# Long convolution in eight channel groups: ScalarE's scaled copy issued one frequency block ahead, VectorE's product ahead of the sums, and the decay table in three transfers

## The chip, the cores and the metric

One NeuronCore of a Trainium2 chip runs the whole program once. The metric is device time in microseconds (us) of one execution; the runs of a kernel are compared by their median. Engines are named as in the profile: PE is TensorE's matmul, PEld its weight load, DVE VectorE, ACT ScalarE, POOL GpSimd, SP the engine that issues most transfers.

## The reference, cut to what matters

The program computes two blocks of a network with long convolutions, attention and experts. The change lies in one part of the first block, the bidirectional long convolution of the first mixer. Its filters are implicit: a small net gives values per position, a last matrix (`f_w4`) and a decay table turn them into taps for each of 2048 channels, forward and backward, and each channel is divided by the sum of the taps' magnitudes.

```python
filt = (hdn @ w4.astype(F32)).reshape(T, 2, D_INNER)
filt = filt * jnp.exp(-t * deltas[None, :])[:, None, :]
filt = filt / (jnp.sum(jnp.abs(filt), axis=(0, 1), keepdims=True) + HY_FILTER_EPS)
...
y = jnp.fft.irfft(jnp.fft.rfft(vf, n=n, axis=1) * jnp.fft.rfft(taps, n=n, axis=0)[None],
                  n=n, axis=1)[:, :T]
return (y + vf * skip.astype(F32)).astype(v.dtype)
```

T is 528 and `v` is the product of two streams that the part before has projected and convolved briefly.

## The kernel before, in words

Everything is float32. A matmul operand is split into a high and a low part (`hi_part` on ScalarE, `lo_part` on VectorE or GpSimd), and three matmuls (`mm3`, lines 93 to 95) stand for one. The Fourier transforms are matmuls with cosine and sine matrices (`mats_h`, `mats_l`), made small by folding the signal and the filter into even and odd halves.

The 2048 channels are worked in eight groups `c` of 256. Within a group there are five frequency blocks `z`; the first four have 128 frequencies, the fifth has 57. For each block TensorE transforms the signal (`signal`), then one piece of the next group's filter product (`taps`), then the filter (`freq`). `tensor_conv` fixes that order, and behind the fifth block come the inverse transforms (`tensor_back`), and the sums for the next group's norm (`tensor_filter_end`, line 1058). A group n = c + 1 has its filter made while group c is transformed: three tiles `i` of positions (128, 128 and 41), each in two steps `m`, six steps in all. All six go through one PSUM bank, so each `taps` waits for the VectorE product `hp` (line 1005) of the step before it.

The names that the later steps touch are:

- `hp`, `vector_filter`, line 1005: VectorE's product of filter and decay table, PSUM to SBUF. The second step of a tile also waits for `abs0` of that tile.
- `abs0` and `abs`, `scalar_filter`: ScalarE's magnitudes of the first and second step. In the trace `abs0` is `sq<-hp`, and `abs` is `dec<-hp`, since it overwrites the decay table. For the first tile ScalarE also halves one row (`hp<-hp`), which the small sum of line 1014 (1 partition, 256 columns) needs.
- `fsum`, `vector_differ`, line 1021: VectorE's sum and difference of the taps of one tile.
- `vector_larger`, line 1027: VectorE's maximum of the two magnitudes.
- `hc`, `scalar_freq`: ScalarE's scaled copy of the transformed filter (in the trace `hc<-ps,wf`). It waits for TensorE's filter transform of that block.
- `prods`, `vector_freq`, line 1198: VectorE's product of signal and filter transform, and behind it the two sums `rr` of lines 1204 and 1205. TensorE's signal transform two blocks later waits for `prods`, since it reuses the bank.
- `Y_h`, `scalar_product`: ScalarE's high part of `rr`; `Y_l` is GpSimd's low part of it. `yh` and `yl` are the same for a finished group of outputs.
- `w4s`, `w4h`, `w4l`: sum and difference of the last matrix's halves (VectorE), high part (ScalarE) and low part (GpSimd), for the filter products two groups ahead.
- `dec`: the decay table of a group, 768 KB, fetched by SP as soon as the norm's sums of the group before are done.

Every engine runs its own list of instructions in the order in which the loops `scalar_conv`, `vector_conv`, `gpsimd_conv` and `tensor_conv` write them. One semaphore per engine counts its steps in this part (`cv.vec`, `cv.act` and so on), so an instruction that waits holds all behind it on its engine. The head of group 0 is made inside the part before (`vector_head`, `scalar_head`).

Of the kernel before, what the change touches and what calls it, by code (L numbers as in the profile page):

```python
# [140 lines left out]
def build(nc, stack, I, C, out):  # L141
# [782 lines left out]
    def sync_conv(e, w):  # L924
        w.wait_ge(*lo_by(HEAD - 2))
        e.dma_start(dec[:], C["dec"][0]).then_inc(*land("dec", 0))
        sync_w4(e, w, 1)
        for c in range(1, 8):
            w.wait_ge("cv.pe", "norm", c - 1)
            e.dma_start(dec[:], C["dec"][c]).then_inc(*land("dec", c))  # L930
            if c < 7:
                sync_w4(e, w, c + 1)
        n = first["hyo", 0]
        filters_over(w)
        sync_weights(e, w, n)
        w.wait_ge("cv.pe", "freq", 7, 4)
        sync_weights(e, w, n + 2)
# [58 lines left out]
    def vector_filter(e, w, c, step):  # L996
# [4 lines left out]
        w.wait_ge("dec", c)  # L1001
# [132 lines left out]
    def tensor_freq(e, w, c, z, part):  # L1134
# [15 lines left out]
        w.wait_ge("left" if z == 4 else "tl")  # L1150
# [76 lines left out]
    def tensor_back_end(e, w, c, h):  # L1227
# [3 lines left out]
        w.wait_ge("left")  # L1231
# [99 lines left out]
    def scalar_conv(e, w):  # L1331
        scalar_unit(e, w, (7, 3, 1), hy_step[7, 3, 1])
        scalar_sums(e, w, 0)
        scalar_w4(e, w, 1)
        for c in range(8):
            for z in range(5):
                if c + z == 0:
                    scalar_freq(e, w, 0, 0)
                if c < 7:
                    scalar_filter(e, w, c + 1, z if z < 4 else 5)  # L1340
                if c + z:
                    scalar_freq(e, w, c, z)
                if c < 7 and z == 4:
                    scalar_turned(e, w, c + 1)
                elif c == 7 and z == 2:
# [16 lines left out]
    def vector_head(e, w, x):  # L1362
# [12 lines left out]
        elif x == (7, 3, 0):  # L1375
# [4 lines left out]
            vector_differ(e, w, 0, 2)  # L1380
            vector_larger(e, w, 0, 2)

    def vector_conv(e, w):
# [3 lines left out]
        vector_w4(e, w, 1)  # L1387
        for c in range(8):
            n = c + 1
            for z in range(5):  # L1390
                if c + z == 0:
                    vector_freq(e, w, 0, 0)
                if c < 7:
                    vector_filter(e, w, n, z if z < 4 else 5)
                    if z in (1, 3):
                        vector_differ(e, w, n, z // 2)
                    if z == 3:
                        vector_filter(e, w, n, 4)
                    elif z == 4:
                        vector_differ(e, w, n, 2)  # L1400
                if c + z:
                    vector_freq(e, w, c, z)
                if c < 7 and z in (1, 3):
                    vector_larger(e, w, n, z // 2)
# [29 lines left out]
    def gpsimd_conv(e, w):  # L1434
# [12 lines left out]
        e.dma_start(tl_x[:], C["tl"]).then_inc(*land("tl"))  # L1447
# [4 lines left out]
        e.dma_start(flat(lf[0][:]), C["lf"][0]).then_inc(*land("left"))  # L1452
        e.dma_start(lb_x[:], C["lb"]).then_inc(*land("left"))
        gpsimd_w4(e, w, 1)
        hyena_over(w)
        e.dma_start(flat(lf[1][:]), C["lf"][1]).then_inc(*land("left"))
# [3013 lines left out]
```

## Time and profile before

| | us |
|---|---|
| median of 3 runs (2398.54 to 2405.86) | 2405.53 |
| the profiled execution | 2406.78 |
| its span | 2405.0 |

The profiled execution is the one whose trace is read below; its time holds 1.8 us that lie outside the span.

| engine | busy us | share of the span |
|---|---|---|
| PE | 2236.0 | 93% |
| PEld | 1855.4 | 77% |
| DVE | 1367.0 | 57% |
| ACT | 1004.5 | 42% |
| POOL | 618.4 | 26% |

The shares are means over the whole program. The long convolution of this change takes the stretch from about 411 to 714 us of the span. In the trace a group of channels starts where its first `vT_h,mats_h` matmul does; the groups 1 to 6 lie between 459.28 and 687.60 us. In a row of the order of time the first number is the start in us from the span's start, the second the duration in us, and brackets hold the idle time of the engine before the row with what ended it.

### The profile page before, as it was taken

The page shows a single profiled execution, that of the slowest core. Times are in us where ns is not written, and L with a number is a line of the kernel's source. Part 1 is how long each engine was busy: PE and PEld are TensorE (multiplying, and loading weights), DVE is VectorE, ACT ScalarE, POOL GpSimd, SP SyncE. Part 2 cuts the span into 40 slices and gives each one's busy share as a digit, 9 for nine tenths or more (in the row PEclk, how much of TensorE's full clock was granted, in tenths as well). Part 3 has the DMA queues.
Part 4 walks back from the last instruction along what each step waited for, and adds up shares of the span by engine and source line. Part 5 has one row for each costly group of instructions (what it writes and reads, how often), then busy time and mean ns, then how long its engine had stood idle before and what let it go on. Part 6 is the DMA issues. An engine that isn't in the chain of part 4 may idle for free.

```text
span 2405.0 us, 36878 instructions
## 1 busy us (share of the span) xinstructions
PE 2236.0 (93%) x15305; PEld 1855.4 (77%) x15305; DVE 1367.0 (57%) x2335; ACT 1004.5 (42%) x1832; POOL 618.4 (26%) x520
## 2 busy tenths in 40 slices
PE   7999999898999989999999989889989999699998
PEld 7999999888999989899999867856776677333332
DVE  4455546788872566666666667789455664411112
ACT  4344334444432455655656553435433432211112
POOL 1111123555541132322323201203220111133331
PEclk9999999899999999999999989999988999799999
DMA  5322332110014223222222224312331143799993
GB/s 182 103 74 88 101 116 79 44 36 19 32 54 135 62 69 82 71 74 78 72 69 80 54 53 102 103 36 75 86 113 49 32 126 116 268 367 376 371 377 145
DMA packets 226337, 274.78 MB, mean 114 GB/s; under 512 B 41192, under 2 KB 193737, under 8 KB 213626
## 3 DMA queue, kind: packets, MB, share of 16 engines
q1 hardware_dynamic: 210330, 256.68, 33.4%
q0 software_dynamic: 15264, 13.65, 1.8%
q8 instruction: 121, 1.98, 0.3%
q10 hardware_dynamic: 576, 2.10, 0.2%
q14 instruction: 46, 0.38, 0.1%
HBM read 305.18 MB, written 23.13 MB: 137 GB/s over the span
## 4 chain that ended last, share of the span: by engine, by line
PE 67%; DVE 17%; ACT 8%; issue 4%; DMA 2%; POOL 1%; SPq 0%; DVEq 0%; POOLq 0%; ACTq 0%
PE ps L93 15%; PE ps L94 14%; PE ps L95 14%; PE ps L4073 7%; PE ps L4116 4%; PE ps L1884 2%; ACT sp L115 2%; ACT whi L99 1%; DVE wlo L103 1%; DVE prods L1198 1%; PE ps L3189 1%; DVE fsum L1021 1%; PE ps L4043 1%; PE ps L3056 1%; DVE p L2182 1%
## 5 line engine op out<-in xcount | busy, mean ns | idle before, releaser
L93 PE MATMUL ps<-hn_h,whi 128*128 128x264 f32 (+2 forms) x2256 | 690.9, 306 | 26.7 <-DVE wlo L103 7.7
L95 PE MATMUL ps<-hn_h,wlo 128*128 128x264 f32 (+2 forms) x2256 | 672.9, 298 | 0.0
L94 PE MATMUL ps<-hn_l,whi 128*128 128x264 f32 (+2 forms) x2256 | 672.5, 298 | 0.0
L93 PEld LDWEIGHTS ps<-hn_h,whi 128*128 128x128 f32 x2256 | 431.4, 191 | 51.9 <-issue 18.2
L94 PEld LDWEIGHTS ps<-hn_l,whi 128*128 128x128 f32 x2256 | 431.6, 191 | 9.5 <-issue 0.2
L95 PEld LDWEIGHTS ps<-hn_h,wlo 128*128 128x128 f32 x2256 | 430.0, 191 | 11.5
L103 POOL TENSOR_TENSOR wlo<-wraw,whi 128x2048 fp32r<-128x2048 f32 (+1 forms) x44 | 158.3, 3598 | 464.0 <-ACT whi L99 464.0
L99 ACT ACTIVATE whi<-wraw 128x2048 fp32r<-128x2048 f32 (+1 forms) x134 | 202.4, 1511 | 43.9 <-PE ps L95 37.4
L103 DVE TENSOR_TENSOR wlo<-wraw,whi 128x2048 fp32r<-128x2048 f32 (+1 forms) x90 | 172.7, 1919 | 50.3 <-ACT whi L99 50.1
L4073 PE MATMUL ps<-ex_raw,xT 128*64 128x512 f32 x600 | 135.5, 596 | 0.0
L766 DVE SCALAR_TENSOR_TENSOR c<-ub,vec,c 128x528 f32<-128x528 f32 x48 | 45.6, 949 | 122.5 <-ACT c L115 122.5
L4087 DVE SCALAR_TENSOR_TENSOR gt<-gt,ps 128x256 f32<-128x256 f32 x24 | 10.1, 422 | 171.5 <-ACT gt L115 171.5
L4073 PEld LDWEIGHTS ps<-ex_raw,xT 128*64 128x64 f32 x600 | 42.0, 137 | 76.4 <-issue 74.2
L115 ACT ACTIVATE ub<-ps,vec 128x528 f32<-128x528 f32 x48 | 33.7, 701 | 142.6 <-PE ps L95 142.5
L115 ACT ACTIVATE p<-ps,stat 128x528 f32<-128x528 f32 x64 | 44.9, 702 | 107.2 <-DVE stat L2168 107.2
L4116 PE MATMUL ps<-ex_raw,aT 128*64 128x512 f32 x312 | 87.6, 599 | 0.5 <-ACT aT L115 0.5
L2168 DVE TENSOR_REDUCE stat<-ps 128x1 f32<-128x528 f32 x128 | 84.1, 699 | 2.7 <-PE ps L1884 1.7
L115 ACT ACTIVATE gt<-ps 128x256 f32<-128x256 f32 x24 | 9.2, 383 | 161.4 <-PE ps L4073 161.4
L93 PE MATMUL ps<-yh,whi 128*128 128x272 f32 (+1 forms) x256 | 73.2, 286 | 2.4 <-POOL yl L103 2.4
L94 PE MATMUL ps<-yl,whi 128*128 128x272 f32 (+1 forms) x256 | 72.9, 285 | 0.0
L2182 DVE SCALAR_TENSOR_TENSOR p<-p,stat,sp 128x528 f32<-128x528 f32 x60 | 46.1, 769 | 47.0 <-ACT sp L115 47.0
L95 PE MATMUL ps<-yh,wlo 128*128 128x272 f32 (+1 forms) x256 | 72.9, 285 | 0.0
(704 smaller groups left out, 5312.0 us busy)
## 6 DMA issues: line engine op xcount, KB each, us to landing
ex_raw<-in_w_gate_up SPq DMA_DIRECT2D x49, 1024.0 KB, 8.0
wraw<-in_hy_w_in SPq DMA_DIRECT2D x32, 1024.0 KB, 5.6
wraw<-in_da_w_in SPq DMA_DIRECT2D x64, 512.0 KB, 4.3
ex_raw<-in_w_down SPq DMA_DIRECT2D x26, 1024.0 KB, 7.5
wraw<-in_w_gate_up SPq DMA_DIRECT2D x15, 1024.0 KB, 7.5
wraw<-in_w_in SPq DMA_DIRECT2D x14, 1024.0 KB, 5.5
wraw<-in_hy_w_out SPq DMA_DIRECT2D x8, 1024.0 KB, 7.6
wraw<-in_da_w_out SPq DMA_DIRECT2D x8, 1024.0 KB, 8.2
```

The source lines that it names most:

```text
L93: e.matmul(out, lhsT=l[0], rhs=r[0], start=start, stop=False)
L94: e.matmul(out, lhsT=l[0], rhs=r[1], start=False, stop=False)
L95: return e.matmul(out, lhsT=l[1], rhs=r[0], start=False, stop=stop)
L99: return e.activation(hi, src, ACT.Copy, bias=0.0, scale=scale)
L103: return e.tensor_tensor(lo, src, hi.bitcast(F32), ALU.subtract)
L115: return e.activation(out, in_, func, bias=bias, scale=scale, accum_out=accum)
L766: e.scalar_tensor_tensor(cc[:], u[:, 0:T], V["conv_w0"][:, q:q + 1], cc[:], ALU.mult, ALU.add).then_inc(*mark("hy.vec", "tap", x))
L1884: t = e.matmul(sc[m][:, y, 0:264], lhsT=qk[l][c, q], rhs=qk[r][c, ks], start=(l + r == 0), stop=(l == 1))
L2168: e.tensor_reduce(mx[:, m:m + 1], sc[m][:, :, 0:264], AX.XY, ALU.max, negate=True).then_inc(*mark("da.vec", "max", h, i, m))
L2182: e.scalar_tensor_tensor(p[0][:], p[0][:], ls[:, 0:1], p[1][:], ALU.mult, ALU.add).then_inc(*mark("da.vec", "p", h, i))
L4073: t = e.matmul(bank[2 + n % 2][half, :], lhsT=xT[n % 2][:, 4 * g + k, half], rhs=unsplit(c)[:, k, :], start=(g == 0 and k == 0), stop=(g = ...
L4116: t = e.matmul(bank[6 + g][half, :], lhsT=aT[n % 2][:, k, half], rhs=unsplit(c)[:, k, 512 * g:512 * g + 512], start=(k == 0), stop=(k == 1))
```

## The change

In each group ScalarE and VectorE issue the same instructions in another order. On ScalarE `hc` of block z + 1 now stands where `hc` of block z stood, ahead of `Y_h` of block z; `hc` of block 0 comes first in a group. On VectorE `prods` of a block stands directly behind the `hp` of that block's step, ahead of the sums (`vector_differ`) and of the maximum, and the fifth `hp` (tile 2, step 4) comes behind them. The decay table of a group comes in three transfers, one for each tile, each with its own semaphore. The `w4` steps for group 1 move ahead: on VectorE ahead of the third tile's maximum of group 0, on ScalarE ahead of the sums' high parts. The semaphores `tl` and `left` are merged with `mats0` and `mats2`. TensorE's order is the same.

```diff
     def sync_conv(e, w):
         w.wait_ge(*lo_by(HEAD - 2))
-        e.dma_start(dec[:], C["dec"][0]).then_inc(*land("dec", 0))
+        for i in range(3):
+            e.dma_start(dec[:, i], C["dec"][0][:, i]).then_inc(*land(f"dec{i}", 0))
...
         for c in range(1, 8):
             w.wait_ge("cv.pe", "norm", c - 1)
-            e.dma_start(dec[:], C["dec"][c]).then_inc(*land("dec", c))
+            for i in range(3):
+                e.dma_start(dec[:, i], C["dec"][c][:, i]).then_inc(*land(f"dec{i}", c))
...
     def scalar_conv(e, w):
         scalar_unit(e, w, (7, 3, 1), hy_step[7, 3, 1])
+        scalar_w4(e, w, 1)
         scalar_sums(e, w, 0)
-        scalar_w4(e, w, 1)
         for c in range(8):
+            scalar_freq(e, w, c, 0)
             for z in range(5):
-                if c + z == 0:
-                    scalar_freq(e, w, 0, 0)
                 if c < 7:
                     scalar_filter(e, w, c + 1, z if z < 4 else 5)
-                if c + z:
-                    scalar_freq(e, w, c, z)
-                if c < 7 and z == 4:
+                if z < 4:
+                    scalar_freq(e, w, c, z + 1)
+                elif c < 7:
                     scalar_turned(e, w, c + 1)
-                elif c == 7 and z == 2:
+                if c == 7 and z == 2:
                     filters_over(w)
                     scalar_weights(e, w, first["hyo", 0])
                 scalar_product(e, w, c, z)
...
             vector_turned(e, w, 0)
             vector_differ(e, w, 0, 2)
+            vector_w4(e, w, 1)
             vector_larger(e, w, 0, 2)
 
     def vector_conv(e, w):
         for i in range(3):
             vector_sums(e, w, 0, i)
         vector_unit(e, w, (7, 3, 1))
-        vector_w4(e, w, 1)
         for c in range(8):
             n = c + 1
             for z in range(5):
-                if c + z == 0:
-                    vector_freq(e, w, 0, 0)
                 if c < 7:
                     vector_filter(e, w, n, z if z < 4 else 5)
-                    if z in (1, 3):
-                        vector_differ(e, w, n, z // 2)
+                vector_freq(e, w, c, z)
+                if c < 7 and z in (1, 3):
+                    vector_differ(e, w, n, z // 2)
+                    vector_larger(e, w, n, z // 2)
                     if z == 3:
                         vector_filter(e, w, n, 4)
-                    elif z == 4:
-                        vector_differ(e, w, n, 2)
-                if c + z:
-                    vector_freq(e, w, c, z)
-                if c < 7 and z in (1, 3):
-                    vector_larger(e, w, n, z // 2)
+                elif c < 7 and z == 4:
+                    vector_differ(e, w, n, 2)
                 elif c == 0 and z == 0:
                     vector_filter_end(e, w, 0)
```

In the rows of order below the part in brackets names the semaphores that an instruction waits for. Numbers in names tell buffers apart.

ScalarE at the end of a group's third block and in its fourth and fifth, before:

```order
L115 ACTIVATE hc0_140<-ps,wf_105 128x512 [waits s_cv_pe]
L99 ACTIVATE Y_h2_135<-rr1_143 128x512 [waits s_cv_vec]
L115 ACTIVATE dec_121<-hp_119 128x512 [waits s_cv_vec]
L115 ACTIVATE hc1_141<-ps,wf_105 128x512 [waits s_cv_pe]
L99 ACTIVATE Y_h3_136<-rr0_142 128x512 [waits s_cv_vec]
L115 ACTIVATE sq0_64<-hp_119 41x512 [waits s_cv_vec]
L115 ACTIVATE dec_121<-hp_119 41x512 [waits s_cv_vec]
L115 ACTIVATE hc0_140<-ps,wf_105 57x512 [waits s_cv_pe]
L99 ACTIVATE vT_h0_127<-ps 128x512
```

The same place in the change:

```order
L115 ACTIVATE hc1_141<-ps,wf_105 128x512 [waits s_cv_pe]
L99 ACTIVATE Y_h2_135<-rr1_143 128x512 [waits s_cv_vec]
L115 ACTIVATE dec_121<-hp_119 128x512 [waits s_cv_vec]
L115 ACTIVATE hc0_140<-ps,wf_105 57x512 [waits s_cv_pe]
L99 ACTIVATE Y_h3_136<-rr0_142 128x512 [waits s_cv_vec]
L115 ACTIVATE sq0_64<-hp_119 41x512 [waits s_cv_vec]
L115 ACTIVATE dec_121<-hp_119 41x512 [waits s_cv_vec]
L99 ACTIVATE vT_h0_127<-ps 128x512
```

The `hc` of the fifth block (57x512) has moved from behind both magnitudes of the third tile (41x512) to ahead of `Y_h3` and of both.

VectorE from the fourth `hp` of a group to the fifth block's `prods`, before:

```order
L1005 TENSOR_TENSOR hp_119<-ps,dec_121 128x512 [waits s_cv_pe]
L1021 TENSOR_TENSOR fsum1_117<-hp_119 128x512 [waits s_cv_vec]
L1021 TENSOR_TENSOR fsum1_117<-hp_119 128x512
L1005 TENSOR_TENSOR hp_119<-ps,dec_121 41x512 [waits s_cv_vec,s_cv_pe]
L1198 TENSOR_TENSOR prods_132<-ps,hc1_141 128x1024 [waits s_cv_act]
L1204 TENSOR_TENSOR rr0_142<-prods_132 128x256 [waits s_cv_pool,s_cv_vec]
L1205 TENSOR_TENSOR rr0_142<-prods_132 128x256
L1027 TENSOR_TENSOR dec_121<-dec_121,sq0_64 128x512
L1005 TENSOR_TENSOR hp_119<-ps,dec_121 41x512 [waits s_cv_act,s_cv_pe]
L1021 TENSOR_TENSOR fsum2_118<-hp_119 41x512 [waits s_cv_vec]
L1021 TENSOR_TENSOR fsum2_118<-hp_119 41x512
L1198 TENSOR_TENSOR prods_132<-ps,hc0_140 57x1024 [waits s_cv_act]
```

The same place in the change, where the lines stand two further down in the file:

```order
L1007 TENSOR_TENSOR hp_119<-ps,dec_121 128x512 [waits s_cv_act,s_cv_pe]
L1200 TENSOR_TENSOR prods_132<-ps,hc1_141 128x1024 [waits s_cv_vec,s_cv_act]
L1206 TENSOR_TENSOR rr0_142<-prods_132 128x256 [waits s_cv_pool,s_cv_vec]
L1207 TENSOR_TENSOR rr0_142<-prods_132 128x256
L1023 TENSOR_TENSOR fsum1_117<-hp_119 128x512 x2
L1029 TENSOR_TENSOR dec_121<-dec_121,sq0_64 128x512 [waits s_cv_act]
L1007 TENSOR_TENSOR hp_119<-ps,dec_121 41x512 [waits s_cv_vec,s_dec2,s_cv_pe]
L1007 TENSOR_TENSOR hp_119<-ps,dec_121 41x512 [waits s_cv_act,s_cv_pe]
L1200 TENSOR_TENSOR prods_132<-ps,hc0_140 57x1024
L1206 TENSOR_TENSOR rr1_143<-prods_132 57x256 [waits s_cv_pool,s_cv_vec]
```

The fifth `hp` (the first of 41x512) now stands behind `prods`, its two `rr` and the maximum, and directly ahead of the sixth, whose wait for ScalarE is for `sq0_64<-hp_119 41x512` above.

## Rows read from the trace of the kernel before

**Rows 1.** Groups 1 to 6; stretch, us, busy PE PEld DVE ACT POOL, clock, DMA, GB/s

```profile
650.10:687.60 37.50, 34.67 (x271) 33.47 (x272) 31.99 (x46) 16.69 (x28) 18.62 (x22) 0.95 0.07 22
sum 228.32, PE 207.21 PEld 200.79 DVE 192.33 ACT 100.65 POOL 120.70; mean PE 34.54 PEld 33.47 DVE 32.06 ACT 16.78 POOL 20.12
```

**Rows 2.** What TensorE waited for in groups 1 to 6: us, times, longest

```profile
PE ps L985 <- DVE hp L1005: 9.4, 7, 1.5
PE ps L93 <- DVE prods L1198: 8.8, 6, 2.5
```

**Rows 3.** VectorE in group 6, in order of time: start, us, instruction, [idle before]

```profile
654.46 0.69 DVE L1005 TENSOR_TENSOR hp<-ps,dec 128x512 f32<-128x512 f32 x1
...
660.72 1.31 DVE L1014 SCALAR_TENSOR_TENSOR hp<-hp 1x256 f32<-1x256 f32 x1 [1.68 <-ACT hp L115]
...
669.37 0.42 DVE L1205 TENSOR_TENSOR rr<-prods 128x256 f32<-128x256 f32 x1
...
670.42 2.94 DVE L1021 TENSOR_TENSOR fsum<-hp 128x512 f32<-128x512 f32 x2
673.46 0.68 DVE L1005 TENSOR_TENSOR hp<-ps,dec 41x512 f32<-41x512 f32 x1
...
677.44 0.68 DVE L1005 TENSOR_TENSOR hp<-ps,dec 41x512 f32<-41x512 f32 x1 [0.77 <-ACT sq L115]
678.16 1.29 DVE L1021 TENSOR_TENSOR fsum<-hp 41x512 f32<-41x512 f32 x2
679.40 1.22 DVE L1198 TENSOR_TENSOR prods<-ps,hc 57x1024 f32<-57x1024 f32 x1
...
681.33 1.27 DVE L103 TENSOR_TENSOR vT_l<-ps,vT_h 128x512 fp32r<-128x512 f32 x2
```

**Rows 4.** TensorE in group 6: fifth filter product to the next group's start

```profile
674.20 0.32 PE L985 MATMUL ps<-w4h,hdnS 128*41 128x256 f32 x1 [1.44 <-DVE hp L1005]
...
677.86 0.28 PE L1163 MATMUL ps<-fl_x,lf 128*57 128x256 f32 x1
...
687.48 0.36 PE L93 MATMUL ps<-vT_h,mats_h 128*128 128x256 f32 x1
```

**Rows 5.** ScalarE in group 6, fifth frequency block

```profile
676.71 0.63 ACT L115 ACTIVATE sq<-hp 41x512 f32<-41x512 f32 x1
...
678.70 0.67 ACT L115 ACTIVATE hc<-ps,wf 57x512 f32<-57x512 f32 x1
679.27 1.05 ACT L99 ACTIVATE vT_h<-ps 128x512 fp32r<-128x512 f32 x2
```

**Rows 6.** GpSimd in group 6

```profile
660.43 1.32 POOL L103 TENSOR_TENSOR yl<-gg,yh 128x528 fp32r<-128x528 f32 x1
...
667.97 0.18 POOL L1080 COPY fold<-vv 128x2 f32<-128x2 f32 x1
...
669.06 0.44 POOL L1080 COPY fold<-vv 128x2 f32<-128x2 f32 x1
...
671.07 1.74 POOL L103 TENSOR_TENSOR Y_l<-rr,Y_h 128x512 fp32r<-128x512 f32 x1
```

**Rows 7.** VectorE in group 0: its first product, and the small sum alone

```profile
427.19 1.23 DVE L1198 TENSOR_TENSOR prods<-ps,hc 128x1024 f32<-128x1024 f32 x1 [7.08 <-ACT hc L115]
...
433.03 0.41 DVE L1014 SCALAR_TENSOR_TENSOR hp<-hp 1x256 f32<-1x256 f32 x1 [1.21 <-ACT hp L115]
```

**Rows 8.** What TensorE waited for at the conv's start and in group 0

```profile
PE ps L985 <- POOL w4l L103: 3.9, 1, 3.9
PE ps L985 <- DVE hp L1005: 3.4, 1, 3.4
```

**Rows 9.** The decay table's transfers: count, KB each, median us to landing

```profile
dec<-c_dec SPq DMA_DIRECT2D x7, 768.0 KB, 4.9
```

**Rows 10.** TensorE's clock behind an idle stretch in group 3, columns as rows 1

```profile
547.90:551.30 3.40, 1.12 (x9) 1.12 (x10) 3.37 (x6) 0.34 (x1) 0.00 (x0) 1.00 0.00 0
551.30:554.70 3.40, 3.40 (x18) 3.40 (x18) 2.09 (x4) 2.03 (x4) 2.97 (x6) 0.50 0.00 0
```

More of the change, by code:

```diff
@@ L1000, in vector_filter @@
         w.wait_ge("cv.pe", "taps", c, step)
-        w.wait_ge("dec", c)
+        w.wait_ge(f"dec{i}", c)
         hp_free(w, c, i)
@@ L1149, in tensor_freq @@
                 w.wait_ge("cv.vec", "y0", c - 1, z)
-        w.wait_ge("left" if z == 4 else "tl")
+        w.wait_ge("mats2" if z == 4 else "mats0")
         name = "fl" if part else "vT"
@@ L1230, in tensor_back_end @@
         w.wait_ge("cv.pool", "Y", c, 4)
-        w.wait_ge("left")
+        w.wait_ge("mats2")
         for b, slot, k, stop in ((bs, 0, 0, False), (bs, 1, 1, True), (bd, 1, 2, False), (bd, 0, 3, True)):
@@ L1446, in gpsimd_conv @@
         w.wait_ge("hy.vec", "done", (7, 0, 1))
-        e.dma_start(tl_x[:], C["tl"]).then_inc(*land("tl"))
+        e.dma_start(tl_x[:], C["tl"]).then_inc(*land("mats0"))
         w.wait_ge("w.done", HEAD)
@@ L1451, in gpsimd_conv @@
                 e.dma_start(flat(y[1][:, 2 * i - 2:2 * i]), part[:, 1064 * i:1064 * i + 1064]).then_inc(*land(f"mats{i}"))
-        e.dma_start(flat(lf[0][:]), C["lf"][0]).then_inc(*land("left"))
-        e.dma_start(lb_x[:], C["lb"]).then_inc(*land("left"))
+        e.dma_start(flat(lf[0][:]), C["lf"][0]).then_inc(*land("mats2"))
+        e.dma_start(lb_x[:], C["lb"]).then_inc(*land("mats2"))
         gpsimd_w4(e, w, 1)
         hyena_over(w)
-        e.dma_start(flat(lf[1][:]), C["lf"][1]).then_inc(*land("left"))
+        e.dma_start(flat(lf[1][:]), C["lf"][1]).then_inc(*land("mats2"))
         e.memset(Y_h[4][:].bitcast(F32), 0.0).then_inc(*mark("cv.pool", "zero", "Y"))
```

## The prediction

> **What bounds the kernel now.** The change lies wholly in the long convolution, so I read the busy time of its groups of channels first: groups 1 to 6 take 228.32 us, 38.05 each, in which TensorE counts as busy for 34.54 and VectorE for 32.06 [rows 1]. The reader is to see two engines near their limit that run after each other. The waits of TensorE say where: 9.4 us in seven waits for `hp` (VectorE's product of filter and decay, which frees the one bank that filter products use) and 8.8 us in six waits for `prods` [rows 2]; 18.2 us in all, about 3 per group. A change that removed all of them and brought nothing else would win some 18 us there. Then VectorE's order of time in group 6 [rows 3]: it idles 1.68 us ahead of the small sum on `hp` and 0.77 us ahead of the last `hp`, and its fifth `hp` starts at 673.46, 23.4 us after the group's start at 650.10 [rows 1, 3]. That is the instruction to follow: TensorE's last filter product starts 0.74 us behind it, at 674.20, and from there it runs without a wait to the next group's first matmul at 687.48 [rows 3, 4]. So the group's length is the fifth `hp` plus 14.0 us. The granted clock of a group is 0.95, that is one stretch of about 3.4 us at 1.2 GHz [rows 1, 10], 1.7 us lost at most.
>
> **The change, part by part.**
> *`prods` ahead of the sums, `hc` one block ahead.* This removes what it aims at. `prods` of block 1 no longer stands behind the sums, so the 8.8 us of waits for it go [rows 2]. `hc` no longer stands behind `abs0`, so VectorE's idle time ahead of `prods` goes too.
>
> *What is queued behind the moved instructions.* ScalarE's `hc` of block 4 now stands ahead of `Y_h` of block 3 and of `abs0` of the third filter tile, and it waits for TensorE's filter transform of block 4. VectorE's sixth `hp` waits for that `abs0`, in the old order as in the new. In the old order `abs0` was done before that transform had ended; now it is behind it. I work the new chain out from the fifth `hp`: to TensorE's last filter product 0.74 (673.46 to 674.20), to the start of the transform's last matmul 3.66 (to 677.86), its 0.28 and 0.05 for the signal 0.33 [rows 3, 4]; `hc` 0.57 (678.70 to 679.27), `Y_h` 0.60 (taken like the row of `sq`, 0.63, less its overlap), `abs0` to `hp` 0.73 (676.71 to 677.44) [rows 3, 5]; sixth `hp` 0.68, `prods` with its two sums 1.93 (679.40 to 681.33), the sums of the third tile 1.24 (678.16 to 679.40) [rows 3]. Together 10.48 us, where now 7.87 stand (673.46 to 681.33). The tail behind, 6.15 us to the next group (681.33 to 687.48), is VectorE's in both: its lowered pieces, then the outputs that free the banks [rows 3, 4]. So the group's length becomes the fifth `hp` plus 16.6, where it was plus 14.0: 2.6 us lost per group, unless the fifth `hp` comes 2.6 earlier.
>
> *When the fifth `hp` comes.* It now stands behind the third block's `prods` and one `larger` as well. From the group's start: VectorE is free for the first `hp` at 4.4 (654.46) [rows 1, 3]. TensorE's matmuls follow each other at 0.118 us (674.20 to 677.86 are 31 steps) [rows 4]; block 1's transform is 64 of them, so it ends at 7.8, `hc` at 8.4, `prods` with its sums at 10.4. The halved row is ready at 10.55, since `Y_h`, `yh` and `abs` stand ahead of it on ScalarE at some 0.6 us each (0.63 for `sq`) [rows 5]; small sum 0.45 [rows 7], sums 1.24, `larger` 0.6, third `hp` 0.6: 13.5, just in time for the next filter product. `prods` 2 and the fourth `hp` to 16.1; `hc` 3 at 16.6; `prods` 3 to 18.6; sums and `larger` to 20.5. So 20.5 without collisions, and a length of 37.1, 0.9 less than the 38.05 of now.
>
> *Collisions with GpSimd.* VectorE's two sums that start at 670.42 took 2.94 us, those at 678.16 1.29 (of a tile of fewer partitions, same columns), and GpSimd's subtraction beside the former 1.74 instead of the 1.32 of its neighbour [rows 3, 6]. The small sum took 1.31 us beside GpSimd's work, and 0.41 alone [rows 3, 7]. GpSimd's tiny copy took 0.44 beside VectorE's `rr` and 0.18 without [rows 3, 6]. So instructions of VectorE that read SBUF alone and GpSimd's exclude each other, and each meeting costs VectorE up to 1.3 us. The Trainium skill says so outright (SBUF — State Buffer, section "SBUF: two separate sides"): a VectorE instruction with two SBUF inputs and a GpSimd one that reads SBUF take the shared ports for a whole instruction, and the other blocks. By that rule the sum is the 2426 below, without it 2399.5; the trace agrees, 2.94 us against 1.29.
> The new order makes these meetings regular: `Y_h` of block z follows `hc` of block z+1 at once, so GpSimd's subtraction starts 0.6 us behind `hc` while VectorE's `rr` sums come 1.25 behind it. In block 1 `rr` waits 0.6 and its second half 1.25 behind `yl`; this makes the small sum 1.6 late; `larger` waits 1.25 for `Y_l` of block 1; in block 3 `rr` waits 0.6 again. The third `hp` comes 2.8 late and holds TensorE; the fifth `hp` comes at 23.9 (3.4 later than 20.5). In groups 1 to 5 the next filter's first sum (`w4s`) meets `Y_h` of block 4: 1.25 more. Lengths: 23.9 + 16.6 + 1.25 = 41.8 in five groups and 40.5 in group 6, 249.5 in all: **21.2 us more** than 228.3. Bounds: none of the collisions 6 x 37.1 = 222.6 (5.7 less); all and a full stretch of half clock besides in each (below) 10 more than 249.5. I take 249.5, since every collision whose places coincide in the trace did cost.
>
> *The start.* Block 0's filter product of group 1 waited 3.9 us for `w4l` and the second 3.4 us for `hp`, behind `prods` that began only after 7.08 us of idle VectorE [rows 7, 8]. With `w4s`/`w4h` earlier and `hp` first, these 7.3 us can go. But group 0 gets the new late chain: 37.1 against about 32 that TensorE needs alone (37.50 less 1.7 of clock and 3.6 of waits and their restarts), 5.1. Net 2.2 us less; bounds 7.3 less and 1 more.
>
> *Decay table in three transfers.* The whole lands 4.9 us after its issue [rows 9], VectorE is free at 4.4: 0.5 us at most per group, already in the 4.4 above; two more issues on SP stand before loads that nobody awaits. The merged semaphores change no wait: nothing.
>
> Sum against the profiled execution, 2406.8 us: 2406.8 + 21.2 - 2.2 = 2425.8, said as 2426. The median of the runs is 2405.5, 1.3 below; I leave that in the range.
>
> **The rivals.**
> (a) *Faster: the collisions don't bite.* Then the fifth `hp` comes at 20.5, under the 21.45 (38.05 - 16.6) from which on a group gets shorter. 2406.8 - 5.7 - 2.2 = 2399, and with all 7.3 at the start 2394. For it: 18.2 us of waits are there to take [rows 2]. Against it: 2.94 against 1.29 [rows 3].
> (b) *Same: no collisions, but half clock.* An idle stretch of TensorE was followed by 3.4 us at 1.2 GHz [rows 10]; if one such stretch falls into each group where TensorE is waited for, a group is 37.1 + 1.7 = 38.8, six 4.5 more than now: 2406.8 + 4.5 - 2.2 = 2409. Half the collisions and no such stretch give 2413.
> (c) *Slower still: both.* 6 x 1.7 on top of 2426 is 2436. For it: new waits of about 3 us at the third `hp` and the fifth, longer than the idle stretch of rows 10.
>
> **How the numbers follow.** A measurement tells about 0.3% from no change, 7 us: 2398 to 2413. Chances: forecast 0.51, (c) 0.14, (b) 0.20, (a) 0.15. So slower 0.65, same 0.20, faster 0.15. The likeliest case has 2416 to 2432 of its own. For 8 in 10 the range goes from 2399, where (a) begins, to 2438, past (c).
>
> **What would show it.** Right: ScalarE's `abs0` of 41 partitions starts after TensorE's 57-column filter transform has ended; VectorE idles 5 to 6 us ahead of its sixth `hp`; groups 1 to 5 are near 41.8 us; `rr` sums of 1 us and more beside GpSimd; waits for `prods` gone, those for `hp` up to about 3 us; the start shorter by some us. Wrong: groups under 38 us, which with the fifth `hp` before 21.4 would be rival (a); `rr` at 0.42 throughout would fell the collisions; an idle time of 1 us ahead of the sixth `hp` would fell the whole chain.

## The result, and the profile after

| | before | after |
|---|---|---|
| median, us | 2404.41 (4 runs, 2398.54 to 2405.86) | 2441.36 (4 runs, 2438.59 to 2444.48) |
| the profiled execution, its span | 2406.78, 2405.0 | 2438.59, 2436.7 |
| busy PE, DVE, ACT, POOL | 2236.0, 1367.0, 1004.5, 618.4 | 2243.7, 1380.3, 1003.1, 622.9 |

The ratio of the runs is 1.0159, with an interval of 1.0137 to 1.018: the change makes the kernel 37.0 us slower. The forecast had the sign and the place, but 2426, and its range ended at 2438: the time lies 3 us outside.

The groups first, as in [rows 1], now with the columns: stretch, us, busy PE, PEld, DVE, ACT, POOL, granted clock, DMA share, GB/s.

```profile
457.47:504.08 46.61, 39.22 (x271) 37.83 (x271) 33.26 (x48) 16.63 (x28) 21.24 (x23) 0.87 0.07 24
504.08:548.34 44.26, 36.71 (x270) 35.30 (x270) 33.26 (x48) 16.64 (x28) 21.25 (x23) 0.92 0.08 25
548.34:591.08 42.74, 35.64 (x271) 34.24 (x271) 33.30 (x48) 16.63 (x28) 21.29 (x23) 0.94 0.07 25
...
681.65:724.09 42.44, 36.28 (x270) 35.13 (x270) 31.60 (x46) 16.11 (x27) 19.32 (x22) 0.92 0.06 19
sum 266.62, PE 223.34 PEld 215.19 DVE 197.94 ACT 99.28 POOL 125.59; mean PE 37.22 PEld 35.87 DVE 32.99 ACT 16.55 POOL 20.93
```

Groups 1 to 6 take 266.62 us instead of 228.32, which is 38.3 more, and group 1 starts at 457.47 instead of 459.21, 1.7 earlier. (What follows group 6 takes between 1712.6 and 1720.9 us in the traces of this study, whatever the kernel. Here it took 4.8 less than in the trace of before, so the profiled executions lie 31.8 apart and the medians 37.0.) VectorE is busy 0.9 us longer per group, where the group is 6.4 longer. So it isn't work that was added, but waiting, and the granted clock of a group fell with it: 0.87 to 0.94, where it was 0.95.

What TensorE waited for, from 395 to 780 us, that is in the whole part (us, times, longest), against [rows 2, 8]:

```profile
PE ps L987 <- DVE hp L1007: 33.8, 14, 2.9
PE ps L93 <- DVE sq L1264: 6.8, 7, 1.1
PE ps L1060 <- DVE dec L1029: 4.4, 6, 0.7
```

The waits for `prods` are gone, as meant, and so is the one for `w4l`. Those for `hp` are 33.8 us, where the same stretch of before has 12.9, and there are new kinds at a group's end, the two shown and 3.5 us in eight waits for GpSimd's `Y_l`.

VectorE in group 3 of after, in order of time (start, duration, instruction, idle before), is the counterpart of [rows 3]. All lines of the part are 2 higher than before.

```profile
558.48 1.23 DVE L1200 TENSOR_TENSOR prods<-ps,hc 128x1024 f32<-128x1024 f32 x1 [1.19 <-ACT hc L115]
559.74 0.89 DVE L1206 TENSOR_TENSOR rr<-prods 128x256 f32<-128x256 f32 x1
560.55 1.54 DVE L1207 TENSOR_TENSOR rr<-prods 128x256 f32<-128x256 f32 x1
...
563.67 1.75 DVE L1029 TENSOR_TENSOR dec<-dec,sq 128x512 f32<-128x512 f32 x1
565.35 0.68 DVE L1007 TENSOR_TENSOR hp<-ps,dec 128x512 f32<-128x512 f32 x1
...
570.49 0.89 DVE L1206 TENSOR_TENSOR rr<-prods 128x256 f32<-128x256 f32 x1
...
572.84 0.68 DVE L1029 TENSOR_TENSOR dec<-dec,sq 128x512 f32<-128x512 f32 x1
573.44 0.67 DVE L1007 TENSOR_TENSOR hp<-ps,dec 41x512 f32<-41x512 f32 x1
579.97 0.68 DVE L1007 TENSOR_TENSOR hp<-ps,dec 41x512 f32<-41x512 f32 x1 [5.85 <-ACT sq L115]
580.57 1.21 DVE L1200 TENSOR_TENSOR prods<-ps,hc 57x1024 f32<-57x1024 f32 x1
...
583.86 1.36 DVE L958 TENSOR_TENSOR w4s<-w4r 128x256 f32<-128x256 f32 x1
...
585.48 1.28 DVE L103 TENSOR_TENSOR vT_l<-ps,vT_h 128x512 fp32r<-128x512 f32 x2
```

ScalarE and GpSimd beside it:

```profile
578.14 0.68 ACT L115 ACTIVATE hc<-ps,wf 57x512 f32<-57x512 f32 x1 [7.90 <-PE ps L1165]
578.73 0.62 ACT L99 ACTIVATE Y_h<-rr 128x512 fp32r<-128x512 f32 x1
579.25 0.62 ACT L115 ACTIVATE sq<-hp 41x512 f32<-41x512 f32 x1
```

```profile
559.05 1.30 POOL L103 TENSOR_TENSOR Y_l<-rr,Y_h 128x512 fp32r<-128x512 f32 x1 [3.69 <-ACT Y_h L99]
560.30 1.52 POOL L103 TENSOR_TENSOR yl<-gg,yh 128x528 fp32r<-128x528 f32 x1
```

Two things are to be seen. The queueing that the prediction described is there: `hc` of block 4 waits 7.90 us for TensorE, `abs0` (`sq`) stands two places behind it, and the sixth `hp` waits 5.85 for that. And the collisions are at each place that it named: `rr` at 0.89, 1.54 and 0.89 instead of 0.42, the maximum 1.75 instead of 0.68, `w4s` 1.36 instead of 0.41. `prods`, which reads PSUM, keeps its 1.23 us beside `Y_l` (558.48 to 559.71 against 559.05 to 560.35).

The third thing is only seen when the groups are compared. The fifth `hp` starts 25.1 us after the start of group 3, and 27.4 after that of group 1. From the fifth to the sixth `hp` it is 6.53 us in group 3, and 8.07 to 8.09 in the five others. The reason is in the clock. Columns as above; the second row of each pair below is the same stretch of a group, in which TensorE makes the last filter product and the filter transform of block 4. Group 2, group 3, and then the first 3.4 us of group 6 of before:

```profile
504.08:507.48 3.40, 3.40 (x16) 3.40 (x17) 3.37 (x5) 0.48 (x1) 3.34 (x5) 0.51 0.85 290
...
531.28:534.68 3.40, 3.40 (x18) 3.40 (x17) 0.00 (x0) 0.00 (x0) 0.00 (x0) 0.51 0.00 0
```

```profile
548.34:551.74 3.40, 3.40 (x16) 3.40 (x17) 3.37 (x5) 0.48 (x1) 3.34 (x5) 0.51 0.81 280
...
575.54:578.94 3.40, 3.40 (x31) 3.40 (x30) 0.00 (x0) 0.80 (x2) 0.00 (x0) 1.00 0.00 0
```

```profile
650.10:653.50 3.40, 3.40 (x17) 3.40 (x18) 3.37 (x5) 0.45 (x1) 3.34 (x6) 0.53 0.67 222
```

TensorE's wait for the fifth `hp` is 2.79 us long in group 1 and 2.92 in all others. Behind it the clock was at 1.2 GHz for 3.4 us in five groups (0.50 granted from 486.94, 531.32, 620.07, 664.44 and 708.81, in groups 1, 2, 4, 5 and 6, those with 8.07 to 8.09 us); in group 3 it stayed at 2.4 GHz. A group's time at 1.2 GHz is its length times twice what its clock lacks to 1: some 50 us in the six groups (46.61 x 0.26 = 12.1 in the first, 5.1 in the third), where it was 20. A group is not longer by all of this time, but, as an estimate, by half of it at most, since at 2.4 GHz TensorE does the same work in about half the time (31 matmuls in the second stretch of group 3, 18 in that of group 2).

Means over groups 1 to 6 of the traces, one trace for each kernel, in us, measure each experiment below. "Tail" is from the fifth `hp` to the first `vT_l`; from there to the next group's start it is 5.6 to 6.1 in all but one.

| | fifth `hp` after the start | to the sixth `hp` | tail | length | at 1.2 GHz |
|---|---|---|---|---|---|
| before | 23.94 | 3.98 | 8.42 | 38.05 | 3.4 |
| after | 25.81 | 7.82 | 13.03 | 44.44 | 8.3 |
| e1_table | 23.40 | 3.98 | 8.43 | 37.52 | 3.4 |
| e2_scalar | 22.34 | 7.20 | 11.61 | 40.03 | 4.6 |
| e3_vector | 27.90 | 1.84 | 12.12 | 45.62 | 12.0 |
| e4_start | 24.39 | 3.98 | 8.42 | 38.50 | 4.4 |
| f1_hc4 | 27.10 | 1.64 | 11.50 | 44.19 | 9.4 |
| f2_fifth | 21.52 | 6.99 | 11.40 | 38.59 | 3.4 |
| f3_both | 22.68 | 3.98 | 8.57 | 37.27 | 6.2 |
| f4_fill | 25.68 | 6.52 | 11.72 | 43.00 | 5.5 |
| h1_block4 | 24.98 | 8.07 | 12.48 | 44.42 | 10.2 |
| h2_block3 | 22.70 | 6.88 | 12.09 | 40.49 | 8.1 |
| g1_rest | 23.40 | 3.98 | 8.42 | 37.51 | 3.4 |
| g2_third | 22.87 | 3.98 | 8.42 | 36.98 | 2.8 |

### The profile page after: what moved, and what is told of

It is laid out like the page before. It is cut to its first block, busy times and chain, and to the rows that moved or that the text cites. A ratio compares the mean times of both kernels' runs of the same rounds, so it can differ in the third digit from the quotient of the medians.

```text
span 2436.7 us, 36911 instructions
## 1 busy us (share of the span) xinstructions
PE 2243.7 (92%) x15305; PEld 1860.1 (76%) x15305; DVE 1380.3 (57%) x2335; ACT 1003.1 (41%) x1832; POOL 622.9 (26%) x520
## 4 chain that ended last, share of the span: by engine, by line
PE 49%; DVE 12%; ACT 7%; issue 3%; DMA 1%; POOL 1%; SPq 0%; POOLq 0%; DVEq 0%; ACTq 0%
PE ps L93 9%; PE ps L95 9%; PE ps L94 9%; PE ps L4070 7%; PE ps L4113 4%; PE ps L1881 2%; ACT sp L115 2%; ACT whi L99 1%; DVE wlo L103 1%; PE ps L3186 1%; PE ps L4040 1%; PE ps L3053 1%; DVE p L2179 1%; PE ps L3131 1%; PE ps L1891 1%
## 5 line engine op out<-in xcount | busy, mean ns | idle before, releaser
L4084 DVE SCALAR_TENSOR_TENSOR gt<-gt,ps 128x256 f32<-128x256 f32 x24 | 10.1, 421 | 171.4 <-ACT gt L115 171.4
L115 ACT ACTIVATE hc<-ps,wf 128x512 f32<-128x512 f32 (+1 forms) x40 | 27.5, 687 | 156.4 <-PE ps L1165 156.4
```

Source lines behind the costliest of these rows:

```text
L115: return e.activation(out, in_, func, bias=bias, scale=scale, accum_out=accum)
```

## The experiments

**The parts one by one.** Each of these four is the kernel before with one part of the change.

e1_table has the three transfers and the merged semaphores.

```diff
-            e.dma_start(dec[:], C["dec"][c]).then_inc(*land("dec", c))
+            for i in range(3):
+                e.dma_start(dec[:, i], C["dec"][c][:, i]).then_inc(*land(f"dec{i}", c))
```

> The kernel before, with the decay table of each group in three transfers and the semaphores merged, and nothing else. My theory (order of ScalarE and VectorE, not the transfers): 2404 us, within 3 us of before; the first product hp of a group no longer waits for the table (0.7 us at most), for which TensorE rarely waits. Rival (the three transfers cost: two more issues on SP and three completions each group): 1 us or more in each of 7 groups, 2411 or more.

Measured: 2400.46, ratio 0.9975 (0.9959 to 0.9991). The kernel before waits for the whole table at the first `hp` of groups 2, 3 and 5 (0.68, 0.69 and 0.33 us), as here in group 3:

```profile
540.08 0.69 DVE L1005 TENSOR_TENSOR hp<-ps,dec 128x512 f32<-128x512 f32 x1 [0.69 <-DMA dec<-c_dec]
```

With three transfers these waits are gone and all six groups take 37.46 to 37.56 us. So this part wins 0.5 us per group in the mean, the size of the prediction's bound, though not in group 6, from which the prediction worked and where nothing had waited. Not all of it was shown to come from the waits for the table. 1.4 of the 3.1 us that the six groups lose lie in group 4 of before, its longest with 38.9 us, which shows no such wait. In groups 3 and 4 of before TensorE's 3.4 us at 1.2 GHz lie in the middle of the group (from 551.3 and 588.9), beside waits of 2.5 us for `prods`, and not at its start; in e1_table all groups have them at their start. Why the clock fell there and not at the start stays open.

e2_scalar has ScalarE's new order alone, and e3_vector VectorE's.

```diff
         for c in range(8):
+            scalar_freq(e, w, c, 0)
             for z in range(5):
...
-                if c + z:
-                    scalar_freq(e, w, c, z)
-                if c < 7 and z == 4:
+                if z < 4:
+                    scalar_freq(e, w, c, z + 1)
+                elif c < 7:
                     scalar_turned(e, w, c + 1)
```

> The kernel before with ScalarE's new order alone (hc one block ahead, w4 in its old place). My theory: hc of block 4 now stands ahead of abs0 of the third tile, so the sixth hp waits some 5 us for it and a group's length is its fifth hp + 16.6 instead of + 14.0; with the fifth hp at about 23 us a group takes 40 to 41, plus one more stretch at half clock here and there: 2418 to 2430. Rival (the loss comes from VectorE's order, with its prods and maximum ahead of the fifth hp): hc earlier is a gain or nothing, 2400 to 2406.

```diff
                     vector_filter(e, w, n, z if z < 4 else 5)
-                    if z in (1, 3):
-                        vector_differ(e, w, n, z // 2)
-                    if z == 3:
-                        vector_filter(e, w, n, 4)
-                    elif z == 4:
-                        vector_differ(e, w, n, 2)
-                if c + z:
-                    vector_freq(e, w, c, z)
+                vector_freq(e, w, c, z)
                 if c < 7 and z in (1, 3):
+                    vector_differ(e, w, n, z // 2)
                     vector_larger(e, w, n, z // 2)
+                    if z == 3:
+                        vector_filter(e, w, n, 4)
+                elif c < 7 and z == 4:
+                    vector_differ(e, w, n, 2)
```

> The kernel before with VectorE's new order alone (w4 in its old place). My theory: the fifth hp stands behind prods 3 and a maximum and comes about 1.6 us later (25 us after the group's start instead of 23.4), the sixth hp follows at once, GpSimd's work meets VectorE's no more than before; a group is 1 to 2 us longer: 2410 to 2420, less than ScalarE's order alone. Rival (VectorE's order is the main loss): 2420 or more. Rival (prods ahead of the sums is a gain by itself): under 2400.

Measured: e2_scalar 2422.99, 1.0071 (1.0049 to 1.0093), 16 us slower; in its trace groups 1 to 6 are 12 us longer, and group 1 starts 4.6 later. e3_vector 2457.63, 1.0207 (1.0171 to 1.0242), 51 us slower, far above what was expected and above the whole change. VectorE in group 2 of e3_vector:

```profile
537.41 0.67 DVE L1005 TENSOR_TENSOR hp<-ps,dec 41x512 f32<-41x512 f32 x1
539.25 0.68 DVE L1005 TENSOR_TENSOR hp<-ps,dec 41x512 f32<-41x512 f32 x1 [1.17 <-PE ps L986]
545.52 1.22 DVE L1198 TENSOR_TENSOR prods<-ps,hc 57x1024 f32<-57x1024 f32 x1 [5.58 <-ACT hc L115]
...
547.45 1.28 DVE L1021 TENSOR_TENSOR fsum<-hp 41x512 f32<-41x512 f32 x2
548.83 1.33 DVE L956 TENSOR_TENSOR w4s<-w4r 128x256 f32<-128x256 f32 x1
```

With ScalarE's old order the sixth `hp` comes early, but then VectorE idles 5.58 us at `prods` of block 4, and the third tile's sums and `w4s` stand behind it, although their inputs are there. So the tail is 3.7 us longer than before without any `hc` ahead of `abs0`; and since `prods` 1 to 3 each wait for an `hc` behind a magnitude, the fifth `hp` comes 4.0 us later. Part of its 51 us is the clock's: 8.6 us more per group at 1.2 GHz than before, which is at most 4.3 of the 7.6 us by which a group is longer. The two orders are no independent costs: 16 and 51 against 37 for both.

e4_start has the `w4` steps of group 1 at their new places.

```diff
         scalar_unit(e, w, (7, 3, 1), hy_step[7, 3, 1])
+        scalar_w4(e, w, 1)
         scalar_sums(e, w, 0)
-        scalar_w4(e, w, 1)
...
             vector_differ(e, w, 0, 2)
+            vector_w4(e, w, 1)
             vector_larger(e, w, 0, 2)
...
         vector_unit(e, w, (7, 3, 1))
-        vector_w4(e, w, 1)
```

> The kernel before with the earlier w4 steps for group 1 alone. My theory: the wait of 3.9 us for w4l goes, the second one for hp stays in part, since it hangs on prods of block 0 and TensorE's transform ahead of it; 2400 (2397 to 2403). Rival (the wait only moves to hp): 2404.

Measured: 2402.03, 0.9984 (0.9969 to 0.9998). Group 1 starts at 455.6 us, 3.6 earlier, of which later groups give some back (38.50 each). g1_rest is e1_table and e4_start together, with all orders within a group as before:

> The kernel before with the table in three transfers and the earlier w4 steps, all orders of the groups old. If the two gains of 0.25% and 0.16% add, 0.4% below before, 2395; then the new order in blocks 0 to 2 brings nothing, since with it and both of these 2398 was measured. Rival (the gains don't add, and the new order in blocks 0 to 2 brings some of the 2398): 2400 or more.

Measured: 2400.08, 0.9975 (0.9965 to 0.9986), 5.1 us less. The two alone had 6.5 and 4.9 less than the kernel before beside them, and their gains don't add; the traces have 37.51 us for a group and 455.9 for the start of group 1, both gains at once, so the rest is not told from the spread of the runs (2396 to 2404).

**Putting right what the prediction blamed.** These are after with one part of an order put back. f1_hc4 puts `hc` of block 4 behind `Y_h` 3 and both magnitudes of the third tile, which is the queueing of the tail.

```diff
-                if z < 4:
+                if z < 3:
                     scalar_freq(e, w, c, z + 1)
-                elif c < 7:
-                    scalar_turned(e, w, c + 1)
+                elif z == 4:
+                    scalar_freq(e, w, c, 4)
+                    if c < 7:
+                        scalar_turned(e, w, c + 1)
```

> The changed kernel with one thing put back on ScalarE: hc of block 4 behind Y_h 3 and both magnitudes of the third tile, as before. My theory: the sixth hp no longer waits 5.85 us for abs0, but the third tile's sums still stand behind prods 4, so 2 us per group come back (Y_h, abs0, hp out of the chain behind TensorE's transform): groups of 42 instead of 44.4, 2441 - 13 = 2428. Rival (the queueing on ScalarE is the whole loss): the group falls to 38, near 2405. Rival (it is nothing, all of it is the fifth hp): 2438 or more.

Measured: 2440.61, 1.0151 (1.0134 to 1.0168): nothing won. In group 3 of f1_hc4 VectorE reads

```profile
575.39 1.74 DVE L1029 TENSOR_TENSOR dec<-dec,sq 128x512 f32<-128x512 f32 x1
577.05 0.67 DVE L1007 TENSOR_TENSOR hp<-ps,dec 41x512 f32<-41x512 f32 x1
578.90 0.68 DVE L1007 TENSOR_TENSOR hp<-ps,dec 41x512 f32<-41x512 f32 x1 [1.17 <-PE ps L988]
583.93 1.22 DVE L1200 TENSOR_TENSOR prods<-ps,hc 57x1024 f32<-57x1024 f32 x1 [4.35 <-ACT hc L115]
```

The idle time ahead of the sixth `hp` went from 5.85 to 1.17, and 4.35 us stand ahead of `prods` instead, with the same sums behind. And `Y_h` 3 is now free at once, so GpSimd's `Y_l` 3 meets the maximum ahead of the fifth `hp` (1.74 instead of 0.68): TensorE's longest wait for an `hp` is 4.0 instead of 2.9. In the means the tail is 1.5 us shorter and the fifth `hp` comes 1.3 later, so the one gain is paid back by the other. The queueing is real, but taking it away alone wins nothing.

f2_fifth keeps ScalarE's order and gives VectorE its old order in blocks 3 and 4; h2_block3 and h1_block4 do half of that each. f2_fifth and h2_block3 have in block 3

```diff
+                if c < 7 and z == 3:
+                    vector_differ(e, w, n, 1)
+                    vector_filter(e, w, n, 4)
...
                 vector_freq(e, w, c, z)
...
+                elif c < 7 and z == 3:
+                    vector_larger(e, w, n, 1)
```

and f2_fifth and h1_block4 in block 4

```diff
+                if c < 7 and z == 4:
+                    vector_differ(e, w, n, 2)
                 vector_freq(e, w, c, z)
```

> The changed kernel with VectorE's old order in blocks 3 and 4 (sums, fifth hp, then prods 3; third tile's sums ahead of prods 4), ScalarE's new order kept. My theory: the fifth hp stands 3 us nearer to the group's start (prods 3 with its two sums 1.94, a maximum 0.6, ScalarE's hc 3 0.5), TensorE's wait of 2.9 us for it goes, and w4s meets Y_h 4 no more: 4 us per group, about 2441 - 24 = 2417. Rival (collisions and half clock come whatever the order of block 3): 2430 or more.

> The changed kernel with the fifth hp back ahead of prods 3 and the maximum on VectorE, block 4 left as changed. My theory: this is the main part, the fifth hp comes 4.3 us earlier per group as in the kernel with blocks 3 and 4 both old (21.5 instead of 25.8 us after the group's start): 2441 - 26 = 2415. Rival (the two blocks work only together): 2425 or more.

> The changed kernel with the third tile's sums ahead of prods 4 on VectorE, as before, and nothing else put back. My theory: the sums follow the sixth hp in either order, so they stand in the chain in both; only the meeting of w4s with GpSimd's Y_h 4 goes (1.3 us per group in five groups): 2441 - 7 = 2434. Rival (that pair is most of the loss): 2420 or less.

Measured: f2_fifth 2405.97, 1.001 (1.0001 to 1.002); h2_block3 2418.9, 1.0062 (1.0044 to 1.0081); h1_block4 2439.57, 1.0134 (1.0118 to 1.015). Moving the fifth `hp` back ahead of `prods` 3 and the maximum brings 22 of the 37 us by itself: it comes 3.1 us earlier (22.70), and the length falls by 4.0. VectorE in group 3 of h2_block3:

```profile
561.58 0.68 DVE L1007 TENSOR_TENSOR hp<-ps,dec 41x512 f32<-41x512 f32 x1
562.19 1.21 DVE L1200 TENSOR_TENSOR prods<-ps,hc 128x1024 f32<-128x1024 f32 x1
...
568.14 0.68 DVE L1007 TENSOR_TENSOR hp<-ps,dec 41x512 f32<-41x512 f32 x1 [3.34 <-ACT sq L115]
```

The three instructions that were ahead of it (`prods`, its sums, the maximum) now fall into time in which VectorE idled: 3.34 us are left of the 5.85.

The third tile's sums alone (h1_block4) bring nothing that is told from after, and the groups are as long (44.42). There `w4s` no longer meets GpSimd (0.41 us), and the tail is 1.0 shorter in groups with the same 8.07 us to the sixth `hp`; but from `vT_l` to the next group it takes 6.85 instead of 5.60, with TensorE at 1.2 GHz in 3.4 us of that time (0.50 granted from 538.80 in group 2).

With both, the groups fall to 38.59, so that second step is worth 13 us once the first is made, and 2 by the medians without it. Not all of the 13 is the order's. In groups with the same 6.53 us to the sixth `hp` the tail goes from 12.03 to 11.06, which is the meeting of `w4s` again, 1.0 of the 1.9 us per group; and the time at 1.2 GHz goes from 8.1 to 3.4 us per group, which can be worth up to 2.3. The first step has no such help: after and h2_block3 have 8.3 and 8.1 us at 1.2 GHz.

f3_both puts right both, f1_hc4 and f2_fifth; the new order is then left in blocks 0 to 2 alone, with the table and the start:

> Both of these together: the new order in blocks 0 to 2, the old one in blocks 3 and 4, on ScalarE and VectorE. My theory: a group is its fifth hp, at about 22 us, plus 14: 36.5 to 37.5, where the kernel before has 38; 2395 to 2402, below before. Rival (new order in blocks 0 to 2 is itself the loss, by its collisions with GpSimd at rr): 2410 or more.

Measured: 2397.78, 0.9965 (0.9954 to 0.9975), groups of 37.27 us and the tail back at 8.57. This is not told from g1_rest (0.9965 to 0.9986): the new order in blocks 0 to 2 brings little or nothing by itself. The clock has a part in that. Groups 1 and 2 of f3_both:

```profile
456.24:492.35 36.11, 33.87 (x271) 33.44 (x271) 31.96 (x48) 16.28 (x28) 20.59 (x22) 0.96 0.09 30
492.35:529.87 37.52, 35.28 (x272) 35.05 (x271) 32.85 (x48) 17.30 (x29) 20.82 (x24) 0.91 0.09 29
```

Group 1 has 3.3 us at 1.2 GHz, groups 2 to 6 have 6.8 and take 1.4 us more, where g1_rest has 3.4 in each and takes 37.51. So the order can shorten a group, and it looks as if a second stretch at 1.2 GHz took that back in five of six; this is read from one trace, and no experiment took the stretch away. The step from f2_fifth to f3_both, on the same chip, is the price of ScalarE's queue once VectorE's order is right: 8 us, with the tail 2.8 shorter and the fifth `hp` 1.2 later.

**The clock.** f4_fill is after with matmuls added ahead of the fourth and the sixth filter product, where TensorE waits; their results are never read, and nothing is left out.

```diff
+    def tensor_fill(e, w, c, z):
+        b = trans[(c + z) % 2][1]
+        w.wait_ge("cv.act", "hc", c, z - 2)
+        for k in range(18 if z == 3 else 24):
+            e.matmul(b[:, 0:256], lhsT=mats_h[0][:, 0, 0, 0:128], rhs=vTh[0][:, 0, :], start=True, stop=True)
...
                 if c < 7:
+                    if z in (3, 4):
+                        tensor_fill(e, w, c, z)
                     tensor_filter(e, w, c + 1, z if z < 4 else 5)
```

> The changed kernel with matmuls whose result nobody reads put in TensorE's two longest waits of each group (18 ahead of the fourth filter product, 24 ahead of the sixth), into a bank that the next transform overwrites. They take about as long as the waits (2.3 and 2.9 us). Theory that the excess over my sum is half clock: the granted clock in the groups goes from about 0.91 to 0.95 or more, and 10 us or so of the 38 come back: 2428 to 2434. Rival (the clock follows nothing, or its loss lies beside the waits): 2441 or more, since the added matmuls delay what follows.

Measured: 2438.13, 1.0138 (1.0121 to 1.0155), 3 us less than after, which the intervals don't tell from it, and less gain than expected. In the traces groups 1 to 6 are 8.6 us shorter and group 1 starts 5.3 later (462.7). Of the 5.3 us 3.3 arise ahead of the first added matmul, where the two kernels are the same, and so are no effect of it; 2.0 arise in group 0, behind it. The stretch behind the fifth `hp` in group 2 of f4_fill, the counterpart of the one from 531.28 above, and VectorE there:

```profile
533.36:536.76 3.40, 3.40 (x30) 3.39 (x30) 0.00 (x0) 0.00 (x0) 0.00 (x0) 1.00 0.02 5
```

```profile
539.03 0.68 DVE L1007 TENSOR_TENSOR hp<-ps,dec 41x512 f32<-41x512 f32 x1 [5.85 <-ACT sq L115]
```

From the fifth to the sixth `hp` it is now 6.52 or 6.53 us in all six groups, the 6.53 of group 3 of after, where it was 8.07 to 8.09 in the other five. So the 1.55 us were the clock's, and they went when TensorE had no idle time there. The groups' starts stayed at 1.2 GHz, and the fifth `hp` at 25.68.

**A version that beats both.** g2_third is f3_both with the third `hp` ahead of the first tile's maximum.

```diff
-                if c < 7:
+                if c < 7 and z != 2:
                     vector_filter(e, w, n, z if z < 4 else 5)
...
                     vector_differ(e, w, n, 0)
+                    vector_filter(e, w, n, 2)
                     vector_larger(e, w, n, 0)
```

> The kernel with the new order in blocks 0 to 2 alone (2398), and the third hp ahead of the first tile's maximum, which GpSimd's Y_l 1 holds for 1.1 us. Theory that this collision sets TensorE's remaining wait of 2.2 us for the third hp: the wait falls to 0.6 or less, a group from 37.3 to 36, 2390. Rival (the group is set further on, by VectorE's work or by half clock): wait gone, time 2396 to 2400.

Measured: 2395.24, 0.9952 (0.9939 to 0.9966): the lowest median of all, 10 us under before and 46 under after, though its interval overlaps that of f3_both. The third `hp` comes 1.7 us earlier than in f3_both (15.28 against 16.96), but the length falls by 0.3 only, since the fifth `hp` stayed (22.87 against 22.68): the gain went into the second tile's sums, which take 2.95 us where f3_both has 1.69 and a wait of 0.91. Beside g1_rest, on the same chip, it is 4.8 us faster; the intervals only just touch (g1_rest from 0.9965), so that what the order itself brings is not firmly shown.

## Why the prediction was right and where it failed

- *`prods` ahead of the sums ends the 8.8 us of waits.* Right; none is left.
- *`hc` of block 4 ahead of `abs0` makes the sixth `hp` wait.* Right as a row: 5.85 us, within the forecast 5 to 6; from the fifth `hp` to `vT_l` group 3 took 12.04, where 10.48 + 1.25 was worked out. As a cause it was half the truth. f1_hc4 takes this wait away and wins nothing, e3_vector has the long tail without it. VectorE's own new order, `prods` ahead of the third tile's sums, holds the tail up as well, and only both together give it back (f3_both, 8.57).
- *Collisions with GpSimd.* Right at each named place, with 0.5 for `rr` instead of 0.6, and about 1.1 for its second half and the maximum, 0.95 for `w4s`, instead of 1.25. (The prediction's 2399.5 without collisions and the 2399 of rival (a) are one sum, 2398.9.) The Trainium skill (SBUF — State Buffer, section "SBUF: two separate sides") has it that an instruction of VectorE with two inputs in SBUF and one of GpSimd that reads SBUF take the shared ports for a whole instruction. The trace agrees: the two `rr` sums end 0.28 and 0.27 us behind GpSimd's `Y_l` and `yl` (560.63 and 562.09 against 560.35 and 561.82), and `prods`, one of whose inputs is in PSUM, isn't lengthened.
- *The fifth `hp` at 23.9.* This term failed first. It came at 24.9 to 25.1 in four groups and at 27.4 in two. The working let block 1's transform end at 7.8 us by taking all 64 matmuls at 0.118 us, so that `prods` 1 would start at 8.4. It starts at 10.1 (558.48 less 548.34), for the first 3.4 us of a group ran at 0.51: 1.7 us lost. The same was to be read in group 6 of before (650.10:653.50 at 0.53); I had counted that stretch in the group's length, but put it nowhere in the new chain. (Whether it held up the old one as well is not shown.) Three groups show it without. Groups 2 and 3 of f2_fifth and group 6 of g2_third start at full clock; the last two groups of g2_third:

```profile
603.38:640.62 37.24, 34.45 (x271) 33.42 (x270) 33.32 (x48) 16.91 (x28) 21.12 (x23) 0.95 0.10 29
640.62:676.26 35.64, 32.84 (x272) 31.85 (x271) 33.85 (x46) 16.86 (x28) 19.40 (x22) 1.00 0.07 23
```

```profile
649.24 1.22 DVE L1200 TENSOR_TENSOR prods<-ps,hc 128x1024 f32<-128x1024 f32 x1 [0.38 <-ACT hc L115]
```

  In group 6 `prods` 1 starts 8.6 us behind the group's start, near the forecast 8.4, its fifth `hp` at 21.6 instead of 23.1, and it is 1.6 us shorter. In group 2 of f2_fifth, which has the new order in block 1 too, `prods` 1 starts 8.6 behind the start as well (503.73 less 495.13). The fifth `hp` came only 1.1 late in the four groups where 1.7 were lost at the start, so the rest of that chain had been put 0.6 too long.
- *No further stretch at half clock in the likeliest case; rival (c), one in each group, at 0.14.* This is the second term that failed. Such a stretch did come behind the fifth `hp` in five groups (1.55 us each, 7.7) and at the start and around the fourth filter product in groups 1 and 4 (2.3 each, 4.6). With some 7 us for the fifth `hp` in all groups and 3.3 less for the end of a group (5.60 behind `vT_l` in all six groups, where the 6.15 of group 6 of before was taken) and some 1.3 more within the tail, this is the 17.1 us, but for rounding, by which the groups' 266.6 exceed the 249.5 of the sum. Rival (c) had named the mechanism and its condition, new waits of about 3 us; its 2436 was nearest. It should have had the larger chance, and the range some 10 us more.
- *The start: 2.2 less.* Measured 1.7 less. Both halves were of about the size thought, each somewhat larger: TensorE's signal transform of block 2 in group 0 starts 8.3 us earlier (426.73 against 435.01, forecast 7.3), and from there to group 1 it takes 6.5 longer (30.74 against 24.21, forecast 5.1), with the new tail (5.88 us ahead of the sixth `hp`). The `w4` steps alone (e4_start) bring 3.6 of the first.
- *The table: at most 0.5 per group, merged semaphores nothing.* e1_table shows 0.5 per group for the two together.
- *Where one should have looked for the cause.* The sum had the fifth `hp` go from 23.4 to 23.9 and put the loss on ScalarE's queue. The experiments turn this round: with the fifth `hp` back ahead of `prods` 3 (h2_block3), all the rest of the change costs 14 us, and with it behind `prods` 3 and the maximum, 37. Ahead of these, TensorE's last filter product and transform run while VectorE does them; behind them VectorE has nothing to do in that time but wait.

How much of the 37 us is the clock's own is bounded, not settled: 30 us more at 1.2 GHz lose at most 15, and f4_fill gave back 8.6 in the groups. By that estimate the order's own part is at least 22, and h1_block4 and f3_both show that the two are tied together: what an order gave, a stretch at 1.2 GHz took back.

## What to carry to other kernels

In a loop in which two engines take turns, find the one instruction with which the other's last long piece of work begins (here the fifth `hp`) and count what the change puts ahead of it; work whose results nobody awaits yet belongs behind it. An instruction moved ahead so that it is not late can still block its queue when its own input comes late: ask of each moved instruction both who waits for it and what it waits for. When new waits of some us appear, price the clock's slow stretch at each place where it can fall on the new chain, also where it was hidden in the old one.

## What was not expected of the hardware

- The same wait did not always have the same consequence: 2.92 us of idle TensorE at one place of a group was followed by 3.4 us at 1.2 GHz in group 2 and by full clock in group 3 (rows 531.28 and 575.54 above), within one execution. The Trainium skill (TensorE: Matmul & The Clock Gate, section "Part 1: The HAM clock gate (the "warmup" mystery)") says that the same kernel can show different numbers of slow matmuls at its start, from run to run. No run here shows that; the trace shows the like between groups of one execution.
- The second of two `rr` sums was lengthened more than the first (1.54 against 0.89): GpSimd's next instruction begins at 560.30, ahead of the first one's end (560.63), and so got in between the two of VectorE, and the second one ended only behind it.
- A table of 768 KB that lands 4.9 us after its issue as one transfer [rows 9] lands in three of 256 KB of which the median takes 3.0 (3.3 in e1_table), and its first part is there in time in groups 1 to 6. In group 0 of after, where the first `hp` now comes earlier, VectorE waited 1.02 us for it.
- g1_rest has 3.4 us at 1.2 GHz at the start of each of groups 1 to 6, though TensorE's longest wait in all of them is 1.5 us; after, with waits of up to 2.9, has some 5 to 12 in a group.
